# Block inverses of a chunked recurrence: whole levels against two halves of four heads

## The reference, cut to what matters

```python
def step(state, inp):
    r_t, w_t, k_t, v_t, a_t, b_t = inp
    sa = jnp.einsum('bhvk,bhk->bhv', state, a_t)
    state = (state * w_t[:, :, None, :] + sa[..., None] * b_t[:, :, None, :]
             + v_t[..., None] * k_t[:, :, None, :])
    return state, jnp.einsum('bhvk,bhk->bhv', state, r_t)
```

## Time and profile before

| what | us |
|---|---|
| median of 3 runs (lowest, highest) | 3592.68 (3591.19, 3596.99) |
| the profiled execution, device time | 3593.53 |
| its span in the trace | 3591.1 |
| chunk stage, first layer (116.2 to 257.4) | 141.2 |
| chunk stage, second layer (1084.6 to 1223.3) | 138.7 |
| PE busy over the span | 3286.0 (92%) |

### The profile page before, as it was taken

The page is one execution under the profiler, slowest core; times in us unless marked ns, Lnnn a source line. Parts: engine busy times, 40 slices in busy tenths (PEclk is TensorE's granted clock), DMA queues, the critical chain, the costliest instruction groups (busy, mean ns, idle before and its releaser), DMA issues. The chain is left out here.

```text
span 3591.1 us, 52445 instructions
## 1 busy us (share of the span) xinstructions
PE 3286.0 (92%) x21352; PEld 2572.2 (72%) x21352; DVE 1512.2 (42%) x2338; ACT 1164.7 (32%) x1881; POOL 1472.5 (41%) x817
## 2 busy tenths in 40 slices
PE   8789999999897889999997989999999988899998
PEld 6674676788567737867874756788888875578787
DVE  6532265789665233848986126220000022520000
ACT  5223333422342234343223425332112232532221
POOL 4321553455243215534442138434334432745453
PEclk9899999999899999999998999999999999999999
DMA  3001122555120111325542110121121111022222
GB/s 126 2 20 43 64 89 77 183 199 193 53 75 3 38 47 53 100 88 194 194 169 81 36 35 1 48 70 60 59 65 65 59 60 44 1 79 97 88 99 84
DMA packets 75022, 282.10 MB, mean 79 GB/s; under 512 B 8320, under 2 KB 8320, under 8 KB 73888
## 3 DMA queue, kind: packets, MB, share of 16 engines
q1 hardware_dynamic: 74784, 278.76, 22.8%
HBM read 276.62 MB, written 2.10 MB: 78 GB/s over the span
## 5 line engine op out<-in xcount | busy, mean ns | idle before, releaser
L131 POOL TENSOR_TENSOR lows<-ring,highs 128x1024 fp32r<-128x1024 f32 x376 | 936.6, 2491 | 1750.8 <-ACT highs L123 1750.8
L155 PE MATMUL ps<-x_high,highs 128*128 128x512 f32 x1936 | 770.9, 398 | 35.5 <-ACT highs L123 16.9
L158 PE MATMUL ps<-x_low,highs 128*128 128x512 f32 x1936 | 758.5, 392 | 0.0
L123 ACT ACTIVATE highs<-ring 128x1024 fp32r<-128x1024 f32 x376 | 397.4, 1057 | 812.7 <-PE ps L155 435.2
L155 PEld LDWEIGHTS ps<-x_high,highs 128*128 128x128 f32 x1936 | 366.4, 189 | 124.7 <-issue 30.7
L158 PEld LDWEIGHTS ps<-x_low,highs 128*128 128x128 f32 x1936 | 366.1, 189 | 77.7 <-issue 3.5
L2470 DVE TENSOR_TENSOR hidden_scratch<-ps,hidden_scratch 128x512 f32<-128x512 f32 x66 | 39.8, 603 | 551.2 <-PE ps L1856 546.3
L669 PE MATMUL ps<-x_high,lows 128*128 128x512 f32 x1040 | 256.8, 389 | 0.0
L669 PEld LDWEIGHTS ps<-x_high,lows 128*128 128x128 f32 x1040 | 195.2, 188 | 40.5
L163 PE MATMUL ps<-hidden_parts,highs 128*128 128x512 f32 (+1 forms) x528 | 191.3, 362 | 12.0 <-PEq L2403 12.0
L166 PE MATMUL ps<-hidden_parts,highs 128*128 128x512 f32 (+1 forms) x528 | 190.4, 361 | 0.0
(11 more groups left out here) (409 smaller groups left out, 5956.4 us busy)
## 6 DMA issues: line engine op xcount, KB each, us to landing
ring<-in_w SPq DMA_DIRECT2D x402, 512.0 KB, 3.5
merging<-in_ada SPq DMA_DIRECT2D x48, 512.0 KB, 3.5
BR<-in_ada SPq DMA_DIRECT2D x48, 512.0 KB, 3.6
more_tiles<-in_dft SPq DMA_DIRECT2D x2, 2048.0 KB, 7.8
X<-in_xT SPq DMA_DIRECT2D x4, 512.0 KB, 6.6
X<-in_memT SPq DMA_DIRECT2D x2, 1024.0 KB, 4.7
merging<-in_cond SPq DMA_DIRECT2D x4, 512.0 KB, 4.6
out<-xT SPq DMA_DIRECT2D x1, 2048.0 KB, 6.3
```

The source lines that it names most:

```text
L123: nc.scalar.activation(self.high(n), self.chunk(n), ACT.Copy).then_inc(self.hi_made, 1)
L131: nc.gpsimd.tensor_tensor(self.low(n), self.chunk(n), self.high(n).bitcast(F32), ALU.subtract).then_inc(self.lo_made, 1)
L155: mm = nc.tensor.matmul(ps, high, xhigh, start=start, stop=False)
L158: nc.tensor.matmul(ps, high, xlow, start=False, stop=False)
```

## The change

Every level of the inverses is done in two halves, `e` = 0 and `e` = 1. The products of a half are issued together, in the order `c`, then `j`, and increment the semaphore by themselves; ACT copies and DVE adds 256 columns at a time; the waits are per half. `DD` and `DT` get one semaphore per half. Nothing is left out: there are as many products as before. Core of the diff:

```diff
@@ PE, gram and post: two waits in place of one
-                        pe.wait_ge(S("dt"), in_level(q, 0))
+                        for e in range(2):
+                            pe.wait_ge(S(f"dt_half{e}"), in_level(q, 0))
@@ PE, level
                     pe.wait_ge(S("mask"), in_level(q, lv))
-                    pe.wait_ge(S("dd"), inv_count(q, lv - 1))
-                    for j, e, c in PAIRS:
-                        mm = nc.tensor.matmul(MD[ROWS[j], e, c, :], MK[lv][ROWS[j], e, c, :], DD[ROWS[j], e, c, :], start=True, stop=True)
-                    mm.then_inc(S("md"), 1)
+                    for e in range(2):
+                        pe.wait_ge(S(f"dd_half{e}"), inv_count(q, lv - 1))
+                        for c in range(4):
+                            for j in range(2):
+                                mm = nc.tensor.matmul(MD[ROWS[j], e, c, :], MK[lv][ROWS[j], e, c, :], DD[ROWS[j], e, c, :], start=True, stop=True)
+                        mm.then_inc(S("md"), 1)
                     if lv == 1:
                         pe.wait_ge(S("dt0"), q + 1)
                         pe.wait_ge(S("z0_out"), q + 1)
-                    else:
-                        pe.wait_ge(S("dt"), in_level(q, lv - 1))
-                    pe.wait_ge(S("x_out"), in_level(q, lv))
-                    if lv < 5:
-                        for j, e, c in PAIRS:
-                            mm = nc.tensor.matmul(DX[ROWS[j], e, c, :], DT[ROWS[j], e, c, :], XX[ROWS[j], e, c, :], start=True, stop=True)
-                        mm.then_inc(S("dx"), 1)
-                    for j, e, c in PAIRS:
-                        mm = nc.tensor.matmul(DXT[ROWS[j], e, c, :], XX[ROWS[j], e, c, :], DT[ROWS[j], e, c, :], start=True, stop=True)
-                    mm.then_inc(S("dxT"), 1)
+                    for e in range(2):
+                        if lv > 1:
+                            pe.wait_ge(S(f"dt_half{e}"), in_level(q, lv - 1))
+                        pe.wait_ge(S("x_out"), 2 * in_level(q, lv) - 1 + e)
+                        if lv < 5:
+                            for c in range(4):
+                                for j in range(2):
+                                    mm = nc.tensor.matmul(DX[ROWS[j], e, c, :], DT[ROWS[j], e, c, :], XX[ROWS[j], e, c, :], start=True, stop=True)
+                            mm.then_inc(S("dx"), 1)
+                        for c in range(4):
+                            for j in range(2):
+                                mm = nc.tensor.matmul(DXT[ROWS[j], e, c, :], XX[ROWS[j], e, c, :], DT[ROWS[j], e, c, :], start=True, stop=True)
+                        mm.then_inc(S("dxT"), 1)
@@ ACT, level
-                    act.wait_ge(S("md"), in_level(q, lv))
-                    if lv > 1:
-                        act.wait_ge(S("dxT"), in_level(q, lv - 1))
-                    a.activation(XX, MD, ACT.Copy).then_inc(S("x_out"), 1)
+                    for e in range(2):
+                        act.wait_ge(S("md"), 2 * in_level(q, lv) - 1 + e)
+                        if lv > 1:
+                            act.wait_ge(S("dxT"), 2 * in_level(q, lv - 1) - 1 + e)
+                        a.activation(XX[:, e], MD[:, e], ACT.Copy).then_inc(S("x_out"), 1)
@@ DVE, gram_low
-                        ins = v.tensor_tensor(DD[:, e], DD[:, e], mask_of("eye"), ALU.add)
-                        ins.then_inc(S("dd") if e else S("dd_half"), 1)
+                        v.tensor_tensor(DD[:, e], DD[:, e], mask_of("eye"), ALU.add).then_inc(S(f"dd_half{e}"), 1)
@@ DVE, level
-                    if lv < 5:
-                        dve.wait_ge(S("dx"), 4 * q + lv)
-                        v.tensor_tensor(DD, DD, DX, ALU.add).then_inc(S("dd"), 1)
-                    dve.wait_ge(S("dxT"), in_level(q, lv))
-                    v.tensor_tensor(DT, DT, DXT, ALU.add).then_inc(S("dt"), 1)
+                    for e in range(2):
+                        if lv < 5:
+                            dve.wait_ge(S("dx"), 2 * (4 * q + lv) - 1 + e)
+                            v.tensor_tensor(DD[:, e], DD[:, e], DX[:, e], ALU.add).then_inc(S(f"dd_half{e}"), 1)
+                        dve.wait_ge(S("dxT"), 2 * in_level(q, lv) - 1 + e)
+                        v.tensor_tensor(DT[:, e], DT[:, e], DXT[:, e], ALU.add).then_inc(S(f"dt_half{e}"), 1)
```

More of the change, by code:

```diff
@@ L1025, in level @@
                         pe.wait_ge(S("z0_out"), q + 1)
-                    else:
-                        pe.wait_ge(S("dt"), in_level(q, lv - 1))
-                    pe.wait_ge(S("x_out"), in_level(q, lv))
-                    if lv < 5:
-                        for j, e, c in PAIRS:
-                            mm = nc.tensor.matmul(DX[ROWS[j], e, c, :], DT[ROWS[j], e, c, :], XX[ROWS[j], e, c, :], start=True, stop=True)
-                        mm.then_inc(S("dx"), 1)
-                    for j, e, c in PAIRS:
-                        mm = nc.tensor.matmul(DXT[ROWS[j], e, c, :], XX[ROWS[j], e, c, :], DT[ROWS[j], e, c, :], start=True, stop=True)
-                    mm.then_inc(S("dxT"), 1)
+                    for e in range(2):
[11 more added lines that the diff above has]
+                        mm.then_inc(S("dxT"), 1)
                 def post(q):
-                    pe.wait_ge(S("dt"), in_level(q, 5))
+                    for e in range(2):
+                        pe.wait_ge(S(f"dt_half{e}"), in_level(q, 5))
                     pe.wait_ge(S("tok"), 8)
```

## The result

| | before | after |
|---|---|---|
| median, us (lowest to highest, runs) | 3592.39 (3591.19 to 3596.99, 4) | 3556.8 (3554.9 to 3560.07, 4) |
| ratio, 95% interval | 1 | 0.990 (0.9882 to 0.9917) |
| profiled execution, span | 3591.1 | 3553.2 |
| chunk stage, first layer | 141.20 | 124.09 |
| chunk stage, second layer | 138.74 | 123.28 |

The kernel is 35.6 us (1.0%) faster; the forecast was 3563 in a range of 3556 to 3582. Of the 37.9 us by which the spans of the two profiled executions differ, 32.6 lie in the two chunk stages.

What follows compares the result with a forecast made beforehand. PE was taken to wait in a chain of product, copy, product, addition, each engine waiting for whole tiles. 34 us gained, less 1.5 for waits and 2.9 for the clock, gave 30: 3563 us, range 3556 to 3582.

Steps and rivals of the forecast that it cites:

- The levels: Levels 3 and 4 with nothing between: start to start falls from 3.98 to 3.14 us; level 5 to post 0.99 less.
- The cover: ACT and DVE: half-size copies (0.38 us) and additions (0.42 us) stay hidden behind PE's issue.
- The margin of 0.15: Levels 3 and 4: DD's second half is ready at 3.46 us, the next level wants it at 3.61.
- (a): PE gets at most three more waits a level; 1.5 us taken for 120 waits, upper bound 18.
- (b): More ACT and DVE instructions: 0.16 and 0.15 us more per whole tile, hidden by PE's issue.
- (c): Before the first transposes PE idles 3.4 us instead of 1.99; a low-clock spell expected in both layers, 2.9 us lost.
- The sum: Whole kernel: 34 us from the steps, less 1.5 for waits and 2.9 for the clock, 30 us gained.
- A: Rival, 0.10: products in opposite PE quarters writing one bank get serialised; a half takes 0.95 us, total 3648.
- B: Rival, 0.08: each added PE wait costs what a release costs, 0.15 us; 18 us instead of 1.5, total 3579.
- C: Rival, 0.05: ACT starts only after both halves of MD; DX at 1.73 us, 0.49 later in 38 levels, total 3581.

Runs made afterwards that it cites:

- e2: Changed kernel, but ACT copies MD whole after both halves; products and additions stay in halves: 3588.98 us, ratio 0.9984.
- e3: Changed kernel, but DVE adds whole after both halves of DX or DXT; products and copies stay in halves: 3565.53 us, ratio 0.9922.
- e6: Changed kernel with 896 more long-satisfied waits on PE, four behind each half of each product set: 3569.69 us, ratio 0.993.
- e4: Changed kernel without any edit, measured and profiled again: 3562.68 us, ratio 0.9911.
- e1: Kernel before, with only the order of products changed to the new one; sets, copies and additions stay whole: 3595.13 us, ratio 1.0003.
- e5: Changed kernel, but in level 1 PE's first half of MD waits for both halves of DD: 3563.13 us, ratio 0.991.
- e7: Changed kernel with the KE and BE multiplications cut by blocks of 128 positions and spread, BE turned first: 3550.83 us, ratio 0.9878.
- e8: e7 plus the first half of the UP products issued before W1: 3551.8 us, ratio 0.9884.

## Why the prediction was right, and where it was off

**The levels.** Right, each within 0.1 us (the table of steps). The reason is shown and not only argued: e2 puts back the copy alone and e3 the additions alone, and the level goes to 3.79 and 3.73, where the same prices gave 3.85 and 3.73.

**The cover.** The half-size copies and additions, 0.38 and 0.42 each, stayed behind PE's issue, as the timeline shows. The margin of 0.15 held in the levels counted as clean; in some others it can't be told from the stops below.

**(a) The waits.** I took 1.5 us for 120 waits at 0.0125 on average. By e6 they would cost some 1.3, but the cost isn't spread evenly: nothing between sets that are issued without a stop, single stops elsewhere, and perhaps 0.15 at each of four `gram` (e6). The price was right as a size, not as a price of each wait.

**(b) More instructions on ACT and DVE.** Nothing, as forecast.

**(c) The clock.** This step failed. I charged 2.9: a spell of the first layer's price in the second layer. The idle time grew as forecast (3.4 forecast, 3.56 measured), but in the measured profile no spell followed it in the second layer, and in the first it lasted 3.4 us instead of 6.8. There the way from the transposes to level 3 takes 139.73 - 133.22 = 6.51, against 5.29 without a spell: 1.2 us, where the kernel before lost 2.65. So in place of 2.9 lost, 1.4 was gained. With e4 the spell does come in the second layer too, and at 1.2. That it could come in both layers was so; that it always would, and its price, were wrong. Nor is it shown that the change shortened the spell in the first layer: e1, with the kernel before's idle time of 2.0 there, has one of 3.4 us as well (133.40 to 136.81), and e2 has 6.8 in both layers.

Of the ten profiles eight still have the four multiplications ahead of the transposes. In the first layer PE was idle for 1.99 to 3.56 and the spell began less than 1 us behind it in all eight. In the second layer it did so in three (e2, e4, e6); in three (before, after, e3) there was none; in two (e1, e5) a spell began with level 1 itself, behind 2.0 us of idle time there, and the slower level left no idle time ahead of the transposes in e1 and 1.46 in e5. In e7 and e8, which do not have the wait, no spell began in the first pair behind its transposes, in any of the four stages.

**The sum.** 34.2 by the clean steps and 1.4 for the clock are 35.6; the stages gave 32.6. So 3.0 were lost where I had taken 1.5, and most of it has a place:

- 1.7 lie between `gram` and level 2. The six later pairs take 10.24, 10.24, 10.41, 10.53, 11.12 and 11.19, not 10.24 each; before they take 11.73 to 11.81 and once 12.29. Before, level 1 started 6.99 to 7.08 behind `gram` in all six, since it waited for the second identity addition, and that wait hid small stops of PE ahead of it. Now it starts as soon as `kv` is issued, 6.03 to 6.96 behind `gram`, and the stops count.
- 0.7 are stops in single levels, most of them in the second layer's third pair: level 3 to 4 takes 3.55 there and level 4 to 5 3.29.
- 0.5 lie between `post` and the next `gram`, which is 1.60 instead of 1.46 in four places (the 0.15 told of under e6).

The trace names nothing that PE waits for in most of the stops; their cause stays open. What the added waits cost is somewhere in these 3.0 and in the steps, so it is no term beside them.

**What lies outside.** The other 5.3 us of the 37.9 lie outside the two stages, where the program is the same, and are not shown to come from the change. What is left of the span without the stages is 3311.2 before and 3305.8 after, and 3310.9, 3311.8, 3309.2, 3307.3, 3308.5, 3306.9, 3307.1 and 3306.1 in e1 to e8. The same program alone moves by as much in its parts: between the stages 827.0 after and 822.8 in e4, behind them 2363.0 and 2369.0. Still, the three runs with the longest stages also have the most left over, and why is open.

**Luck.** 3556.8 lies only 0.8 inside the near end of the range, 3556. Against the working the clock came out 4.3 better and the time outside the stages 5.3, the stops 1.5 worse, and none of these has to do with the levels. The same program took 3562.68 in e4, next to the 3563 of the forecast. What is solid is the gain of the clean steps, 34.2 against 34.

**The rivals.** A is refuted by e1 (0.95 for 32 records, ratio 1.0003), B by e6, C by `DX` at 1.23 to 1.26 behind `MD` in level 4 and, in the first pair, in levels 2 to 4 (1.32 in level 3, 1.40 and 1.42 in levels 2 and 1 of the later pairs), where C had 1.73. Ahead of `gram` a single wait may cost what B says (0.15), in four places and not in 120.

## What to carry to other kernels

Where engines pass one tile round in a chain, find in the timeline which engine's issue would fill the round if nobody waited: here six half sets at 0.47, 2.8 of 3.98 us. Cut the tile so that this engine's issue becomes as good as continuous (two halves gave 3.11, with 0.28 left ahead of `DX`), and cut the copy first, since no other product of a level can start before it; the smaller instructions cost more per element, which is free as long as they stay behind the issue. Then look at the wait that the table shows next: here one of 3.6 us, caused by the way in which a side product was cut, and worth some 8 us with its clock spells. And a wait that is taken away may have hidden small delays ahead of it: count on less than the clean steps give (3.0 of 35.6 here).

## What the runs showed of the hardware

- Two fp32 products in a row in opposite quarters of PE that write the same PSUM bank in different partitions go as fast as with different banks: 0.95 for 32 records either way (e1).
- A semaphore wait that is long satisfied costs PE about 0.011 us on average (e6 against e4, one profile each), and nothing within a run of products issued without a stop (e6: 24 more in a level of 3.11). Ahead of `gram` one more wait goes with 0.15 us more (0.25 to 0.26 instead of 0.10 behind ACT's copy), but the kernels compared differ in the size of the additions too.
- An idle PE does not always lower its clock: behind the same 3.56 us of idle time, in the same program and place, the granted clock was 1.00 once and at the low level (1.97 for 1.15) the other time (second layer, first profile and e4). This spell of 3.4 us cost 1.2 us. Nor does the idle time fix its length: behind 2.0 us in the first layer it lasted 6.8 in the kernel before and 3.4 in e1.
